# SwiGLU gate/up in a hybrid decoder step: seven-product scheme with chained PSUM accumulation

## The chip, the cores and the metric

The kernel runs on one core of one Trainium2 chip. The metric is the device time of one execution in microseconds, as the median over runs. Engines are called by their names or as the profile abbreviates them: TensorE (PE for matmuls, PEld for its weight loads), VectorE (DVE), ScalarE (ACT), GpSimd (POOL) and SyncE (SP), which issues the DMAs.

## The reference, cut to what matters

One decoder layer over 2048 prompt tokens and 8 sample tokens, width D = 1024, all in fp32. The change touches only the middle of its second half, the gate and up products of the feed-forward block:

```python
def swiglu(h, w_gate, w_up, w_down):
    return (jax.nn.silu(h @ w_gate) * (h @ w_up)) @ w_down
xp = xp + swiglu(rmsnorm(xp, norm2_g[l]), w_gate[l], w_up[l], w_down[l])   # D_FF = 2816
```

## The kernel before, in words

The program is a chain of stages with a barrier between them: input projections, attention, output projection (`combine`), gate and up (`gate_up`, line 2363 on), and down (`down`). Each stage hands the engines their own instruction streams; within a stage everything is ordered by semaphores written out by hand.

**Seven products for eight.** `gate_up` computes each block product by a Strassen-Winograd scheme. The 2056 tokens are split into three passes (`WIDTHS` 344, 344, 340, each for two halves of tokens), the 1024 inputs into two halves, and the output columns are taken two blocks of 128 at a time. One *item* g is such a pair of column blocks of w_gate (even g) or of w_up (odd g): 22 items a pass, 66 in all. An item has seven products, each a 512-deep sum: b11, b21 and b22 use blocks of the weights as they are, t1 to t4 use sums and differences of blocks, made by GpSimd (`combos`, lines 2545 to 2556). The token side uses four blocks and the combinations S1 to S4. Each operand is split in two fp32r parts, hi (a ScalarE copy) and lo (a VectorE or GpSimd difference), and a product is hi*hi + hi*lo + lo*hi: 12 matmuls of 128x344 (lines 2826 to 2828), so 84 an item.

**What is made of them.** With p1 = b11, u2 = p1 + t2, u3 = u2 + t3 and u4 = u2 + t1, the four output quarters are c11 = p1 + b21, c22 = u3 + t1, c21 = u3 + t4 and c12 = u4 + b22. Before, each product has a PSUM bank of its own, taken in turn from eight (`product_bank`). ScalarE copies b11 out of PSUM (line 2647, p1, double buffered); VectorE makes u2 (line 2747), u3 (2757), u4 (2766) and the quarters (2699), every one with one PSUM input. For a gate item ScalarE turns the quarters into silu of them (2656 to 2662). For an up item VectorE multiplies each quarter by the gate's (2703) and makes three sums and two differences for the down stage (2712 to 2720); SyncE then stores them, three or four DMAs of sums (2530) and as many of quarters (2533).

**The order of the queues.** TensorE goes through the items in `ORDER`; every product waits, one item behind, for the reader of the bank that it takes over. In iteration g ScalarE does `base_hi(g+1)` (the hi parts of plain blocks, which waits for item g-1 to be over), the p1 copy, `combos_hi(g+1)` (line 2600, waits for GpSimd's t_made), then the silus of a gate item. VectorE does u2, `combos_lo(g+1)` (2677), `base_lo(g+1)` (2687), u3 and the quarters. GpSimd does `base_lo(g+1)` (2567, 2570, 2571) and `combos(g+2)`, which waits for VectorE's `combos_lo(g+1)`. Before a gate item's c11 VectorE waits for the stores of the sums of the pair before (sum_stored), before an up item's first quarter for those of its quarters (stored).

**The turns.** In the last item of a pass (g = 21 and 43) the token operands are exchanged: ScalarE makes seven new hi parts (`tokens_hi`, line 2632), VectorE seven lo parts (`tokens_lo`, line 2692) between its other work, and GpSimd the last combination S4 (line 2472). SyncE loads the raw tokens of the next pass in item 5 of a pass (`load_tokens`, line 2315, four DMAs of 680 to 688 KB), in its queue between the weight loads and the stores of that item.

**The start.** For item 0 the hi and lo parts are made within the stage. ScalarE's loop over items begins only after all seven token parts, so the p1 copy of item 0 comes after `base_hi(1)`. The weight combinations of item 1 lie in the tile `lead`, whose end is also u3.

The numbers of `T` in this text: T(g) is the start of the first matmul of item g.

Of the kernel before, what the change touches and what calls it, by code (L numbers as in the profile page):

```python
# [25 lines left out]
P = 128  # L26
# [2221 lines left out]
ORDER = ("b11", "t2", "t3", "t1", "b21", "t4", "b22")  # L2248
SLOT = {"t2": 0, "t3": 1, "t1": 2, "t4": 3}
# [113 lines left out]
def gate_up(nc, c, io, scratch, raw, stock, lead):  # L2363
# [20 lines left out]
    with ExitStack() as ctx:  # L2384
# [4 lines left out]
        first = stock[:, 12 * FW + 5 * D - 2 * W:12 * FW + 5 * D].rearrange("p (b t) -> p b t", b=2)  # L2389
# [3 lines left out]
        u2 = sb("u2", [P, 2, W])  # L2393
# [5 lines left out]
        source_of = (A11, S2, S3, S1, A12, A22, S2)  # L2399
        names = ("w_in0 w_in1 t_step t_made t_hi t_lo b_hi b_lo d_lo a11_in h_in s_step h_hi h_lo b_first done p1 u2 u3 u4 c22 c11 c21 c12 silu "  # L2400
                 "quarter summed act stored sum_stored s_stored ahead t2_hi t2_lo tail_in tail_var tail_rooted root_out root_in tail_turned tail_step tail_out")
        with stage(nc, names) as (block, s):
            w_in = (s.w_in0, s.w_in1)

            def source(sc, m):

                return part[:, source_of[m] if sc or m < M - 1 else A11, :, 0:WIDTHS[sc]]
# [25 lines left out]
            def product_bank(g, name):  # L2433
                return ps[:, (M * g + ORDER.index(name)) % 8, :]
# [18 lines left out]
            def s_combo(eng, sc, name):  # L2453
# [14 lines left out]
                else:  # L2468

                    eng.wait_ge(s.s_step, step + 3)  # L2470
                    eng.wait_ge(s.h_lo, M * sc + 1)
                    eng.tensor_tensor(x[S2], x[A12], x[S2], ALU.subtract).then_inc(s.s_step, 1)
# [114 lines left out]
            def _(act):  # L2587
                def combos_hi(g):
# [6 lines left out]
                    if g == 0:  # L2595
                        act.activation(w_hi[0][:, 0], combo[:, 0], ACT.Copy).then_inc(s.t2_hi, 1)
# [22 lines left out]
                def tokens_hi(sc, m):  # L2619

                    n = WIDTHS[sc]
                    if sc and m == 6:
                        act.wait_ge(s.s_step, 4 * sc)
                    elif sc and m == 0:
                        act.wait_ge(s.a11_in, 16 * sc)
                    elif sc and m in (4, 5):
                        act.wait_ge(s.h_in, 48 * sc)
                    elif sc:
                        act.wait_ge(s.s_step, 4 * sc - 4 + {1: 2, 2: 3, 3: 1}[m])
# [3 lines left out]

                combos_hi(0)
                for m in (2, 3):
                    tokens_hi(0, m)
                base_hi(0)
                for m in range(4, M):
                    tokens_hi(0, m)
                for g in range(N):  # L2640
                    n, b = width(g), g % 2
                    if g + 1 < N:
                        base_hi(g + 1)
                    act.wait_ge(s.done, done(g, "b11"))
                    if g >= 2:
                        act.wait_ge(s.c11, g - 1)
                    act.activation(first[:, b, 0:n], product(g, "b11"), ACT.Copy).then_inc(s.p1, 1)
                    if g + 1 < N:
                        combos_hi(g + 1)
                    if is_up(g):  # L2650
                        if g % ITEMS == ITEMS - 1 and g // ITEMS + 1 < SC:
                            for m in range(M):
                                tokens_hi(g // ITEMS + 1, m)
                        continue
                    act.wait_ge(s.c22, g + 1)
                    act.activation(sil[:, 3, 0:n], sil[:, 3, 0:n], ACT.Silu).then_inc(s.silu, 1)
                    act.wait_ge(s.c11, g + 1)
                    act.activation(sil[:, 0, 0:n], sil[:, 0, 0:n], ACT.Silu).then_inc(s.silu, 1)
                    act.wait_ge(s.c21, g + 1)
                    act.activation(sil[:, 1, 0:n], sil[:, 1, 0:n], ACT.Silu).then_inc(s.silu, 1)  # L2660
                    act.wait_ge(s.c12, g + 1)
                    act.activation(sil[:, 2, 0:n], sil[:, 2, 0:n], ACT.Silu).then_inc(s.silu, 1)
# [695 lines left out]
```

## Time and profile before

| what | us |
|---|---|
| runs, median of 3 (lowest, highest) | 2722.22 (2721.59, 2729.13) |
| profiled execution, span from first to last instruction | 2721.9 |
| TensorE matmul busy | 2609.9 (96%) |
| VectorE, GpSimd, ScalarE busy | 1878.3, 1726.6, 1196.8 |
| the gate/up stage, first to last matmul | 1366.2 to 2263.1 |
| mean granted TensorE clock | 0.988 of full |

The profile gives no device time of the profiled execution apart from its span. Matmuls are pipelined: a 128x344 matmul is shown as 320 ns, but one starts every 157 ns, so a stretch in which "PE busy" equals its length has no hole, and a hole shows as missing busy time or as a matmul that starts late. The granted clock (PEclk) is a share of 2.4 GHz; at half of it the matmuls start every 287 ns.

### The profile page before, as it was taken

The page shows a single profiled execution, that of the slowest core. Times are in us where ns is not written, and L with a number is a line of the kernel's source. Part 1 is how long each engine was busy: PE and PEld are TensorE (multiplying, and loading weights), DVE is VectorE, ACT ScalarE, POOL GpSimd, SP SyncE. Part 2 cuts the span into 40 slices and gives each one's busy share as a digit, 9 for nine tenths or more (in the row PEclk, how much of TensorE's full clock was granted, in tenths as well). Part 3 has the DMA queues.
Part 4 walks back from the last instruction along what each step waited for, and adds up shares of the span by engine and source line. Part 5 has one row for each costly group of instructions (what it writes and reads, how often), then busy time and mean ns, then how long its engine had stood idle before and what let it go on. Part 6 is the DMA issues. An engine that isn't in the chain of part 4 may idle for free. (4 is left out here: it accounts for less than half of the span.)

```text
span 2721.9 us, 42328 instructions
## 1 busy us (share of the span) xinstructions
PE 2609.9 (96%) x14706; PEld 2358.5 (87%) x14706; DVE 1878.3 (69%) x2513; ACT 1196.8 (44%) x2106; POOL 1726.6 (63%) x1004
## 2 busy tenths in 40 slices
PE   8999999989999998899989999999999998999998
PEld 7999898877787777787789998999999997888887
DVE  5366687488888888632387888787887784455564
ACT  4222321377777778744453334333433332232343
POOL 3387687489999999665656776677656660222232
PEclk9999999999999999999999999999999999999999
DMA  6588898666667677775636343534345536755564
GB/s 207 176 257 253 265 293 290 180 181 183 177 179 192 184 181 181 237 259 184 200 106 174 115 132 114 173 115 132 114 124 149 154 106 200 245 171 178 182 228 139
DMA packets 471718, 497.17 MB, mean 183 GB/s; under 512 B 173179, under 2 KB 360566, under 8 KB 470474
## 3 DMA queue, kind: packets, MB, share of 16 engines
q1 hardware_dynamic: 450722, 468.96, 57.4%
q10 hardware_dynamic: 20496, 24.45, 2.6%
q8 instruction: 118, 1.93, 0.3%
q0 software_dynamic: 288, 1.05, 0.1%
q14 instruction: 94, 0.77, 0.1%
HBM read 397.06 MB, written 94.16 MB: 180 GB/s over the span
## 5 line engine op out<-in xcount | busy, mean ns | idle before, releaser
L2826 PE MATMUL ps_gate_up<-h_hi,w_hi 128*128 128x344 f32 (+1 forms) x1584 | 509.0, 321 | 15.4 <-DVE h_lo L2692 14.6
L2827 PE MATMUL ps_gate_up<-h_lo,w_hi 128*128 128x344 f32 (+1 forms) x1584 | 507.2, 320 | 0.0
L2828 PE MATMUL ps_gate_up<-h_hi,w_lo 128*128 128x344 f32 (+1 forms) x1584 | 506.6, 320 | 0.0
L2826 PEld LDWEIGHTS ps_gate_up<-h_hi,w_hi 128*128 128x128 f32 x1584 | 299.1, 189 | 18.3 <-DVE h_lo L2692 16.5
L2828 PEld LDWEIGHTS ps_gate_up<-h_hi,w_lo 128*128 128x128 f32 x1584 | 299.4, 189 | 0.0
L2827 PEld LDWEIGHTS ps_gate_up<-h_lo,w_hi 128*128 128x128 f32 x1584 | 299.1, 189 | 0.0
L881 PE MATMUL ps_proj<-w_hi,h_lo 128*128 128x428 f32 (+1 forms) x800 | 284.6, 356 | 0.0
L1601 DVE TENSOR_TENSOR split_halves<-ps_turned,split_halves 128x512 fp32r<-128x512 f32 (+1 forms) x352 | 210.7, 614 | 65.3 <-ACT split_halves L1485 62.9
L3020 POOL TENSOR_TENSOR stock<-common 128x512 f32<-128x512 f32 x55 | 84.0, 1537 | 264.7 <-DMA common<-in_w_down 264.6
L2551 POOL TENSOR_TENSOR stock<-common 128x512 f32<-128x512 f32 x64 | 103.4, 1616 | 230.5 <-DVE w_lo L2677 230.5
L3222 PE MATMUL ps_down<-wd_hi,split_halves 128*128 128x512 f32 x616 | 241.1, 391 | 7.3 <-DVE wd_lo L3130 7.2
L3223 PE MATMUL ps_down<-wd_lo,split_halves 128*128 128x512 f32 x616 | 240.5, 390 | 0.0
L3224 PE MATMUL ps_down<-wd_hi,act_lo 128*128 128x512 f32 x616 | 240.3, 390 | 0.0
L1485 ACT ACTIVATE split_halves<-ps_turned 128x512 fp32r<-128x512 f32 (+1 forms) x352 | 185.8, 538 | 110.9 <-PE ps_turned L1424 96.6
L3068 ACT ACTIVATE split_halves<-stock 128x768 fp32r<-128x768 f32 (+2 forms) x114 | 83.2, 776 | 302.5 <-PE ps_down L3224 288.6
L1424 PE MATMUL ps_turned<-ident,probs 128*128 128x128 f32 x1216 | 195.3, 278 | 15.7 <-DVE split_halves L1601 9.9
L3146 DVE TENSOR_TENSOR acc<-acc,ps_down 128x512 f32<-128x512 f32 x96 | 62.3, 684 | 201.3 <-PE ps_down L3224 201.3
L1424 PEld LDWEIGHTS ps_turned<-ident,probs 128*128 128x128 f32 x1216 | 144.7, 142 | 59.9 <-DVE split_halves L1601 23.1
L2677 DVE TENSOR_TENSOR w_lo<-stock,w_hi 128x2048 fp32r<-128x2048 f32 x64 | 158.9, 2483 | 24.4 <-ACT w_hi L2600 24.4
L528 POOL TENSOR_TENSOR stock<-stock,q_row 128x2048 f32<-128x2048 f32 x32 | 156.5, 4896 | 28.4 <-DMA stock<-in_cache_k 28.3
L730 DVE TENSOR_REDUCE part_scores<-stock 128x32 f32<-128x2048 f32 x48 | 109.4, 2285 | 88.7 <-POOL stock L528 88.1
L1333 POOL TENSOR_TENSOR common<-common,lead 128x2048 f32<-128x2048 f32 x43 | 156.1, 3631 | 18.6 <-DMA common<-in_cache_v 18.6
(407 smaller groups left out, 7280.0 us busy)
## 6 DMA issues: line engine op xcount, KB each, us to landing
stock<-in_cache_k SPq DMA_DIRECT2D x192, 256.0 KB, 3.5
common<-in_cache_v SPq DMA_DIRECT2D x172, 256.0 KB, 3.1
stock<-act_combined SPq DMA_DIRECT2D x56, 704.0 KB, 4.3
common<-in_w_gate SPq DMA_DIRECT2D x33, 1024.0 KB, 5.3
common<-in_w_up SPq DMA_DIRECT2D x33, 1024.0 KB, 6.8
common<-in_w_down SPq DMA_DIRECT2D x44, 512.0 KB, 5.9
page_v<-in_cache_v SPq DMA_DIRECT2D x84, 256.0 KB, 3.0
common<-in_w_in SPq DMA_DIRECT2D x44, 428.0 KB, 4.7
```

The costliest lines, as they stand in the source:

```text
L528: pool.tensor_tensor(part, part, query, ALU.mult).then_inc(s.pool_done, 1)
L881: mm = pe.matmul(ps[:, bank, 0:w], a_lo, w_hi[:, d, :], start=False, stop=(j == 3 and d == 1))
L1424: turned = pe.transpose(out[:, r * P:(r + 1) * P], probs(u.head, QCH * u.ch + r, u.j * P, (u.j + 1) * P), c.ident[:])
L1485: act.activation(a.p_hi[:, m % PARTS, r0 * P:], ps_t[:, bank_of["unit", m], r0 * P:], ACT.Copy).then_inc(s.t_hi, 1)
L1601: dve.tensor_tensor(a.p_lo[:, m % PARTS, r0 * P:], ps_t[:, bank_of["unit", m], r0 * P:], a.p_hi[:, m % PARTS, r0 * P:].bitcast(F32), ALU.s ...
L2677: dve.tensor_tensor(shape(w_lo[g % 2][:, 0:4]), shape(combos_second if g == 1 else combo), shape(w_hi[g % 2][:, 0:4]).bitcast(F32), ALU.su ...
L2826: pe.matmul(acc, a_hi, h_hi[:, d, :], start=d == 0, stop=False)
L2827: pe.matmul(acc, a_hi, h_lo[:, d, :], start=False, stop=False)
L2828: mm = pe.matmul(acc, a_lo, h_hi[:, d, :], start=False, stop=d == H - 1)
L3222: pe.matmul(out, a_hi[:, n % 2, j, :], w_hi[:, slot, :], start=first, stop=False)
L3223: pe.matmul(out, a_hi[:, n % 2, j, :], w_lo[:, slot, :], start=False, stop=False)
L3224: mm = pe.matmul(out, a_lo[:, n % 2, j, :], w_hi[:, slot, :], start=False, stop=end)
```

## The change

The products come in another order, and sums that VectorE made are left to the accumulation in PSUM: t2 is added onto the bank of b11, t3 onto that of t2, and b22 onto that of t1. ScalarE copies the bank of b11 out three times: after b11 (p1), after t2 (u2) and after t3 (u3). The sum u4 is gone, since t1 + b22 now comes out of one bank. Items take bank 0 to 3 or 4 to 7 in turn. p1 is single now. A product that adds onto a bank waits for the reader of the same item: t2 for p1, t3 for u2, b22 for VectorE's c22. The other four wait two items behind. In the last item of a pass the token parts are spread between the p1, u2 and u3 copies on ScalarE, and on VectorE from ahead of `combos_lo` to the end. For a gate item the wait for sum_stored now stands ahead of c11 and c22, and c11 comes first. The token combination S4 is written to another part (A11).

```diff
-ORDER = ("b11", "t2", "t3", "t1", "b21", "t4", "b22")
+ORDER = ("b11", "t1", "t2", "b21", "t3", "t4", "b22")
+BANK = {"b11": 0, "t2": 0, "t3": 0, "t1": 1, "b22": 1, "b21": 2, "t4": 3}
+ADDS = {"t2": "b11", "t3": "t2", "b22": "t1"}
...
-                return ps[:, (M * g + ORDER.index(name)) % 8, :]
+                return ps[:, 4 * (g % 2) + BANK[name], :]
...
# ScalarE
                     act.wait_ge(s.done, done(g, "b11"))
-                    if g >= 2:
-                        act.wait_ge(s.c11, g - 1)
-                    act.activation(first[:, b, 0:n], product(g, "b11"), ACT.Copy).then_inc(s.p1, 1)
+                    if g >= 1:
+                        act.wait_ge(s.c11, g)
+                    act.activation(p1[:, 0:n], product(g, "b11"), ACT.Copy).then_inc(s.p1, 1)
+                    if turn:
+                        tokens_hi(turn, 0)
                     if g + 1 < N:
                         combos_hi(g + 1)
+                    act.wait_ge(s.done, done(g, "t2"))
+                    if g == 0:
+                        act.wait_ge(s.t_lo, 2)
...
+                    act.activation(u2[b][:, 0:n], product(g, "t2"), ACT.Copy).then_inc(s.u2, 1)
+                    if turn:
+                        for m in (1, 2):
+                            tokens_hi(turn, m)
+                    act.wait_ge(s.done, done(g, "t3"))
+                    if g >= 1:
+                        act.wait_ge(s.c21, g)
+                    act.activation(u3[:, 0:n], product(g, "t3"), ACT.Copy).then_inc(s.u3, 1)
+                    if turn:
+                        for m in range(3, M):
+                            tokens_hi(turn, m)
...
# VectorE
-                    dve.tensor_tensor(u2[:, b, 0:n], product(g, "t2"), first[:, b, 0:n], ALU.add).then_inc(s.u2, 1)
                     if g + 1 < N:
                         combos_lo(g + 1)
                         base_lo(g + 1)
+                    if turn:
+                        tokens_lo(turn, 1)
...
-                    dve.tensor_tensor(u3[:, 0:n], u2[:, b, 0:n], product(g, "t3"), ALU.add).then_inc(s.u3, 1)
...
+                    else:
+                        dve.wait_ge(s.sum_stored, stored_before(q))
+                    dve.wait_ge(s.p1, g + 1)
+                    quarter(g, "b21", p1[:, 0:n], 0, s.c11)
+                    dve.wait_ge(s.u3, g + 1)
                     quarter(g, "t1", u3[:, 0:n], 3, s.c22)
-                    dve.tensor_tensor(u2[:, b, 0:n], u2[:, b, 0:n], product(g, "t1"), ALU.add).then_inc(s.u4, 1)
...
# TensorE
-                        if m == 0 and g >= 2:
-                            pe.wait_ge(s.c12, g - 1)
-                        if m >= 1:
-                            pe.wait_ge((s.p1, s.u2, s.u3, s.u4, s.c11, s.c21)[m - 1], g)
+                        if name in ADDS:
+                            pe.wait_ge({"t2": s.p1, "t3": s.u2, "b22": s.c22}[name], g + 1)
+                        elif g >= 2:
+                            pe.wait_ge({"b11": s.u3, "t1": s.c12, "b21": s.c11, "t4": s.c21}[name], g - 1)
...
-                            pe.matmul(acc, a_hi, h_hi[:, d, :], start=d == 0, stop=False)
+                            pe.matmul(acc, a_hi, h_hi[:, d, :], start=d == 0 and name not in ADDS, stop=False, skip_group_check=name in ADDS)
```

## Rows read from the trace of the kernel before

**Rows 1.** The page's first part: busy time of each engine over the span.
```profile
PE 2609.9 (96%) x14706; PEld 2358.5 (87%) x14706; DVE 1878.3 (69%) x2513; ACT 1196.8 (44%) x2106; POOL 1726.6 (63%) x1004
```

**Rows 2.** Windows: stretch, length, busy us of PE, PEld, DVE, ACT, POOL, clock, DMA.
```profile
1660.00:1680.00 20.00, 13.29 (x65) 12.24 (x64) 19.69 (x19) 6.42 (x7) 10.98 (x5) 0.78 0.16 51
...
1700.00:1900.00 200.00, 200.00 (x1277) 200.00 (x1276) 159.05 (x207) 73.50 (x103) 138.74 (x87) 1.00 0.49 144
...
1960.00:1980.00 20.00, 12.35 (x68) 11.26 (x66) 19.69 (x19) 7.14 (x7) 11.72 (x5) 0.91 0.15 49
```

**Rows 3.** Timeline of TensorE: first matmul of items 0, 1, 6, 20, 21, 23.
```profile
1366.23 0.63 PE L2826 MATMUL ps_gate_up<-split_halves 128*128 128x344 f32 x1 [6.00 <-PEq L84]
1382.90 0.32 PE L2826 MATMUL ps_gate_up<-split_halves,w_hi 128*128 128x344 f32 x1
1450.14 0.32 PE L2826 MATMUL ps_gate_up<-split_halves 128*128 128x344 f32 x1
1635.69 0.32 PE L2826 MATMUL ps_gate_up<-split_halves 128*128 128x344 f32 x1
1648.87 0.32 PE L2826 MATMUL ps_gate_up<-split_halves,w_hi 128*128 128x344 f32 x1
1686.08 0.32 PE L2826 MATMUL ps_gate_up<-split_halves,w_hi 128*128 128x344 f32 x1
```

**Rows 4.** Groups by line in the stage: busy us, mean ns; idle before.
```profile
L2747 DVE TENSOR_TENSOR u<-ps_gate_up,stock 128x344 f32<-128x344 f32 (+1 forms) x66 | 33.8, 511 | 99.3 <-PE ps_gate_up L2828 78.3 <-ACT stock L2647 21.1
L2757 DVE TENSOR_TENSOR lead<-u,ps_gate_up 128x344 f32<-128x344 f32 (+1 forms) x66 | 33.1, 501 | 0.9 <-PE ps_gate_up L2828 0.9
L2766 DVE TENSOR_TENSOR u<-u,ps_gate_up 128x344 f32<-128x344 f32 (+1 forms) x66 | 33.1, 501 | 0.0
L2647 ACT ACTIVATE stock<-ps_gate_up 128x344 f32<-128x344 f32 (+1 forms) x66 | 29.4, 445 | 8.2 <-PE ps_gate_up L2828 8.2
```

**Rows 5.** Timeline of item 29 (up): its first matmul; ScalarE; VectorE.
```profile
1765.16 0.32 PE L2826 MATMUL ps_gate_up<-split_halves,w_hi 128*128 128x344 f32 x1
1767.94 0.43 ACT L2647 ACTIVATE stock<-ps_gate_up 128x344 f32<-128x344 f32 x1
1768.27 1.91 ACT L2600 ACTIVATE w_hi<-stock 128x2048 fp32r<-128x2048 f32 x1
1772.73 0.68 DVE L2687 TENSOR_TENSOR w_lo<-common,w_hi 128x512 fp32r<-128x512 f32 x1
1783.87 0.52 DVE L2720 TENSOR_TENSOR lead<-lead 128x344 f32<-128x344 f32 x1
```

**Rows 6.** Timeline of the stage's start: ScalarE's first p1 copy, VectorE's `combos_lo(1)`.
```profile
1378.19 0.46 ACT L2647 ACTIVATE stock<-ps_gate_up 128x344 f32<-128x344 f32 x1
1380.49 4.00 DVE L2677 TENSOR_TENSOR w_lo<-lead,w_hi 128x2048 fp32r<-128x2048 f32 x1
```

**Rows 7.** Timeline around item 6: token loads, stores of sums, VectorE's c11 quarter.
```profile
1448.43 5.62 SPq L2315 DMA_DIRECT2D stock<-h_turned  x4
1456.95 3.09 SPq L2530 DMA_DIRECT2D act_combined<-lead  x3
1465.67 0.51 DVE L2699 TENSOR_TENSOR lead<-stock,ps_gate_up 128x344 f32<-128x344 f32 x1 [4.13 <-DMA act_combined<-lead]
```

**Rows 8.** Timeline of the first turn: TensorE, VectorE, ScalarE, GpSimd.
```profile
1670.29 0.42 PE L2826 MATMUL ps_gate_up<-h_hi,w_hi 128*128 128x344 f32 x1 [4.20 <-DVE h_lo L2692]
1675.92 0.65 PE L2826 MATMUL ps_gate_up<-h_hi,w_hi 128*128 128x344 f32 x1 [2.52 <-DVE h_lo L2692]
1665.43 3.29 DVE L2712 TENSOR_TENSOR lead<-lead 128x344 f32<-128x344 f32 x1
1684.99 0.68 DVE L2687 TENSOR_TENSOR w_lo<-common,w_hi 128x512 fp32r<-128x512 f32 x1
1664.99 3.36 POOL L2472 TENSOR_TENSOR stock<-stock 128x1376 f32<-128x1376 f32 x1
1671.11 0.43 ACT L2647 ACTIVATE stock<-ps_gate_up 128x344 f32<-128x344 f32 x1
```

More of the change, by code:

```diff
@@ L2641, in _ @@
                     n, b = width(g), g % 2
+                    turn = g // ITEMS + 1 if g % ITEMS == ITEMS - 1 and g // ITEMS + 1 < SC else 0
                     if g + 1 < N:
@@ L2650, in _ @@
+                    act.wait_ge(s.done, done(g, "t3"))
[3 more added lines that the diff above has]
+                    if turn:
+                        for m in range(3, M):
+                            tokens_hi(turn, m)
                     if is_up(g):
-                        if g % ITEMS == ITEMS - 1 and g // ITEMS + 1 < SC:
-                            for m in range(M):
-                                tokens_hi(g // ITEMS + 1, m)
@@ L2662, in _ @@
-                    act.activation(sil[:, 2, 0:n], sil[:, 2, 0:n], ACT.Silu).then_inc(s.silu, 1)
+                    gated(g, 0, s.c11)
+                    gated(g, 3, s.c22)
+                    gated(g, 1, s.c21)
+                    gated(g, 2, s.c12)
             @block.vector
@@ L2734, in _ @@
                 combos_lo(0)
-                for m in (2, 3):
-                    tokens_lo(0, m)
+                tokens_lo(0, 2)
                 base_lo(0)
-                for m in range(4, M):
+                for m in range(3, M):
                     tokens_lo(0, m)
@@ L2750, in _ @@
                         base_lo(g + 1)
[L2751 removed]
+                    if turn:
+                        tokens_lo(turn, 1)
                     if g == 1:
                         sample_turned()
[L2754 to L2760 removed]
                     if is_up(g):
@@ L2764, in _ @@
                             dve.wait_ge(s.s_stored, 16 * (q - (SC - 1) * PAIRS))
+                    else:
+                        dve.wait_ge(s.sum_stored, stored_before(q))
+                    if g == 0:
+                        dve.wait_ge(s.t_lo, 2)
+                    dve.wait_ge(s.p1, g + 1)
+                    quarter(g, "b21", p1[:, 0:n], 0, s.c11)
+                    dve.wait_ge(s.u3, g + 1)
                     quarter(g, "t1", u3[:, 0:n], 3, s.c22)
-                    dve.tensor_tensor(u2[:, b, 0:n], u2[:, b, 0:n], product(g, "t1"), ALU.add).then_inc(s.u4, 1)
                     if turn:
-                        tokens_lo(turn, 1)
-                    if not is_up(g):
-                        dve.wait_ge(s.sum_stored, stored_before(q))
-                    quarter(g, "b21", first[:, b, 0:n], 0, s.c11)
+                        tokens_lo(turn, 2)
                     if is_up(g):
@@ L2774, in _ @@
                     if turn:
-                        tokens_lo(turn, 2)
+                        tokens_lo(turn, 3)
                     quarter(g, "t4", u3[:, 0:n], 1, s.c21)
@@ L2779, in _ @@
                     if turn:
-                        tokens_lo(turn, 3)
-                    dve.wait_ge(s.u4, g + 1)
-                    quarter(g, "b22", u2[:, b, 0:n], 2, s.c12)
+                        tokens_lo(turn, 4)
+                    dve.wait_ge(s.u2, g + 1)
+                    quarter(g, "b22", u2[b][:, 0:n], 2, s.c12)
                     if is_up(g):
@@ L2785, in _ @@
                     if turn:
-                        for m in range(4, M):
+                        for m in range(5, M):
                             tokens_lo(turn, m)
@@ L2806, in _ @@
                             pe.wait_ge(s.d_lo, 1)
[L2807 removed]
+                        if g == 1 and name == "t1":
                             pe.wait_ge(s.t_lo, 2)
```

78 lines of the change are left out of this document (34 added, 44 removed).

## The prediction

> **What bounds the kernel now.** I began with the page: TensorE is busy 96% of the span, VectorE 69%, ScalarE 44% [rows 1]. The change lies in one stage, so I cut that stage into windows. In the middle of a pass 200 us hold 200.00 us of matmuls while VectorE is busy 159 us and ScalarE 73.5 us: there is no hole, and a matmul starts every 157 ns [rows 2]. An item lasts 13.18 us (item 20 to item 21) [rows 3], so each of its seven products has 1.88 us. Holes lie only where a pass turns: 6.7 and 7.6 us of two windows of 20 us, with VectorE busy 19.7 us of each and a granted clock of 0.78 and 0.91 [rows 2]. The first turn, T(21) to T(23), takes 37.21 us where two items need 26.36 [rows 3]: 10.85 us too many. So TensorE bounds the stage, and VectorE bounds its turns. What is taken from VectorE in mid-pass is worth nothing; the question is whether TensorE's new waits, on the reader of the same item instead of one an item back, are met.
>
> **What the change removes and adds.** It removes u2, u3 and u4 from VectorE, 66 each of 511, 501 and 501 ns [rows 4]: 99.9 us. It adds 132 copies to ScalarE at the 445 ns of the p1 copy [rows 4]: 59 us. The number of matmuls and of TensorE's waits is the same. With no hole in mid-pass, all this is hidden by TensorE, provided that the next part holds.
>
> **Mid-pass: do the three new waits hold?** I take item 29, an up item, from T = 1765.16 [rows 5]. Product k starts at T + 1.88 k (k from 0), and its first weight load 0.2 earlier.
> - t2 (k = 2) is due to start at 3.77, and needs p1. The copy ends at 1768.37, T + 3.21 [rows 5], and nothing ahead of it on ScalarE changes. 0.35 to spare.
> - t3 (k = 4) is due at 7.53 and needs u2. ScalarE is through with `combos_hi` at T + 5.02 [rows 5], t2 is over at 5.9, the copy ends at 6.35. 1.0 to spare.
> - b22 (k = 6) is due at 11.30 and needs c22, which needs u3: t3 over at 9.65, copy to 10.1, c22 to 10.6. VectorE has finished `base_lo` at T + 8.25 [rows 5], does c11 and its product by 9.4, and waits for u3. 0.5 to spare.
>
> In a gate item the wait for the stores comes ahead of c22. VectorE's work of an up item now ends at T(30) + 6.05 (1784.39) [rows 5]; three operations fewer make it some 4.5, so sums land sooner too. I cost mid-pass at 0; the cover is those 0.35 and 0.5 us.
>
> **The start: +7.8 us, and perhaps 1.0 of clock.** In item 0 p1 stands behind all token parts and `base_hi(1)` on ScalarE and ends at 1378.65 [rows 6]. The before kernel doesn't care, because nothing of item 0 needs it; now t2, the third product, waits for it. Next ScalarE's u2 copy waits for t_lo = 2, the end of `combos_lo(1)`: 1380.49 + 4.00 = 1384.49 [rows 6]. So u2 ends at 1384.95, and t3, t4 and b22 follow: 3 x 1.88, T(1) = 1390.7. It was 1382.90 [rows 3]: +7.8. TensorE idles 6.5 us before t2, 2.5 before t3. At a turn the hole of 4.2 us [rows 8] stands in the window with clock 0.78 [rows 2]. At half clock t3, t4 and b22 would add 12 x 130 ns each, 4.7 us; the second turn's 0.91 says less. I take 1.0, bounds 0 and 4.7.
>
> The Trainium skill (TensorE: Matmul & The Clock Gate, Part 1) says that idleness takes the array to half of its 2.4 GHz and only sustained work brings it back. By it the 4.7 would stand in full, and the sum would be 3.7 us higher. The trace agrees in kind (0.78 and 0.91 at the turns), not on the amount.
>
> **What the start gives back: -2.4 us.** Items 1 to 20 take 1648.87 - 1382.90 = 265.97 us, where 20 x 13.18 = 263.6 [rows 3]. The 2.4 us is lost because GpSimd, VectorE and ScalarE run behind TensorE after the start. With TensorE 7.8 us later they are not behind.
>
> **Item 6: +4.1 us.** The token loads occupy SyncE for 5.62 us and the DMA queues for longer. The stores of sums behind them are issued at 1456.95, and VectorE waited 4.13 us for them, to 1465.67 [rows 7], which is T(6) + 15.5 [rows 3]. That hid behind TensorE, as c22 had gone ahead of the wait and only c11 was late. Now c11 and c22 both stand behind it, and b22 of the same item needs c22, due at T + 11.3. The stores may be issued up to 2 us sooner, but the token loads are ahead of them; c11 starts between T + 13.7 and 15.5, b22 1.1 later: 3.5 to 5.3 us of waiting. I take 4.1; the lower bound is 0, should the stores land at once. At item 28 I saw no such wait, and cost it at 0.
>
> **The turns: +0.8 each.** VectorE is the chain. `base_lo(23)` ends at 1685.67, T(21) + 36.8 [rows 8]. Three 0.5 us operations fall out of the chain and it starts 0.5 earlier, with `tokens_lo(0)`: 35.0. But then c11 and c22 of item 22 follow (1.0), and only then may b22 start (1.9): T(23) at T(21) + 37.9, against 37.2. Inside, ScalarE makes a second wait. S4 ends on GpSimd at T(21) + 19.5, the last token part and the p1 copy of item 22 come behind it, to 22.7 [rows 8]. As `tokens_lo(0)` now stands ahead of `combos_lo(22)`, GpSimd starts 1.4 later, and t2 of item 22 can't start before 24.2 (the third product started at 21.4 [rows 8]). At full clock four products bring TensorE to 31.7, in time for c22 at 36.0; at half clock, 3.44 us each, to 38.0, and T(23) would be 4 us late. I take 0.8, 1.6 for both; bounds -4 and +4 a turn.
>
> **The sum.** 7.8 + 1.0 - 2.4 + 4.1 + 1.6 = +12.1 us. The profiled span of 2721.9 becomes 2734.0; the median of the runs is 0.3 above that span. I forecast 2734, 0.4% slower. A measurement of this kernel can tell about 0.3%, 8.2 us, from no change.
>
> **Rivals.**
> - *The mid-pass waits miss.* An operation with both inputs in SBUF takes VectorE 0.52 us alone [rows 5] and 3.29 beside GpSimd [rows 8]. If such lengthening costs c22 more than the 0.5 to spare, by 0.3 to 0.6 us in each of 33 up items, it adds 10 to 20: about 2749. For it: the margin is thin. Against: item 29 already has GpSimd running beside it. Chance 0.12.
> - *The turns at half clock.* 3.2 more at each turn: 2740 and, with a slow start, up to 2745. Chance 0.12.
> - *No change that can be told.* The stores of item 6 land early (-4.1) and the turns gain 1 to 3 us each because VectorE's lengthened operations fall differently beside GpSimd: 2721.9 + 12.1 - 4.1 - 1.6 - 4 = 2724. Chance 0.20.
> - *Faster, by the turns.* VectorE at 19.7 of 20 us is what makes the holes, and the change takes work from just this engine. If its chain shrank until the turns had no hole, they would give back 2 x 10.85: 8.8 - 2.4 + 4.1 - 21.7 = -11.2, 2711. It decides at T(21) to T(23) below 27.9 us; the other terms are +10.5, and 8.2 more must come from two turns. Against it: three operations are 1.5 us, and only contention with GpSimd (3.29 against 0.52) could give the rest. Chance 0.06.
>
> The Trainium skill (SBUF — State Buffer, § Who interferes with whom) says that a VectorE instruction with two SBUF inputs contends with a GpSimd one that reads SBUF, and one with at most one doesn't. The removed operations read one input from PSUM and keep to 0.50 us; by that rule all lengthened ones stay, which speaks against the last rival.
>
> That the change doesn't do what it says would show as adds left on VectorE; the diff leaves none.
>
> **How the numbers follow.** The forecast itself (2728 to 2740) has 0.50. Slower than 2730.4: 0.46 of that and the two slower rivals, 0.70. Within 0.3%: the rest of the forecast and the third rival, 0.24. Faster: 0.06. The range 2724 to 2748 leaves out the faster rival, a part of the third and the worst of the first.
>
> **What would show it.** T(1) near 1390.7, with a hole before item 0's third product that ends with ScalarE's copy, and one before its fifth. A hole of 3.5 to 5.3 us before b22 of item 6. Mid-pass windows still full. T(21) to T(23) near 38, with t2 of item 22 waiting for ScalarE. I am wrong if mid-pass windows show holes, if T(1) moves by less than 6, or if a turn takes under 34 us.

## The result, and the profile after

The changed kernel takes 2746.88 us (median of 5 runs, 2744.22 to 2747.71), the kernel before beside it 2722.22 (2718.83 to 2729.13). The ratio is 1.0093, interval 1.0082 to 1.0105: 24.7 us slower, where 12.1 was forecast. The profiled execution took 2747.01 us with a span of 2745.3.

The page's first part, after:
```profile
PE 2620.0 (95%) x14706; PEld 2366.1 (86%) x14706; DVE 1803.7 (66%) x2315; ACT 1254.4 (46%) x2238; POOL 1715.0 (62%) x1004
```
Against [rows 1] VectorE lost 74.6 us of busy time, ScalarE gained 57.6. The work moved as meant; that bought nothing. Added up one by one, VectorE's operations in the stage fell by 90.0 us and not by the 99.9 of the three groups, since others got longer, above all its products with the gate's quarters (115.4 to 146.8 us). The page counts time in which two operations overlap once, and so shows less still.

The window in mid-pass of [rows 2], after (columns as there), then the first turn:
```profile
1700.00:1900.00 200.00, 198.08 (x1253) 197.23 (x1253) 137.01 (x155) 84.13 (x127) 129.22 (x85) 0.99 0.46 135
1662.00:1700.00 38.00, 27.85 (x152) 26.49 (x151) 32.91 (x27) 17.49 (x20) 21.82 (x12) 0.89 0.30 88
```
The first line matters: 1277 matmuls before, 1253 after. TensorE has holes in mid-pass, though VectorE is less busy (137 for 159 us).

First matmuls of items 0, 1, 6, 7, 21 and 23, after, which answer to [rows 3]:
```profile
1362.66 0.63 PE L2840 MATMUL ps_gate_up<-split_halves 128*128 128x344 f32 x1 [6.17 <-PEq L84]
1387.47 0.32 PE L2840 MATMUL ps_gate_up<-split_halves,w_hi 128*128 128x344 f32 x1
1453.79 0.32 PE L2840 MATMUL ps_gate_up<-split_halves 128*128 128x344 f32 x1
1473.28 0.39 PE L2840 MATMUL ps_gate_up<-split_halves,w_hi 128*128 128x344 f32 x1
1659.01 0.32 PE L2840 MATMUL ps_gate_up<-split_halves,w_hi 128*128 128x344 f32 x1
1699.98 0.49 PE L2840 MATMUL ps_gate_up<-split_halves,w_hi 128*128 128x344 f32 x1
```
T(g) is again the start of the first matmul of item g, T1-T0 the time from T(0) to T(1). Over all 66 items, in sections, each row from the one profiled execution of its kernel (us; e1 to e9 are the experiments below; "stage" is from the start of the first to the start of the last matmul of gate and up):

| | T1-T0 | T21-T1 | T23-T21 | T43-T23 | T45-T43 | T65-T45 | stage |
|---|---|---|---|---|---|---|---|
| before | 16.7 | 266.0 | 37.2 | 263.6 | 36.9 | 263.2 | 896.6 |
| after | 24.8 | 271.5 | 41.0 | 268.3 | 40.4 | 264.8 | 923.8 |
| e1 | 24.7 | 267.9 | 38.9 | 263.6 | 39.9 | 263.6 | 911.6 |
| e2 | 23.4 | 271.4 | 40.6 | 267.2 | 40.7 | 264.0 | 920.3 |
| e3 | 24.7 | 271.6 | 37.8 | 269.0 | 38.2 | 265.9 | 920.1 |
| e4 | 24.8 | 271.9 | 39.5 | 267.0 | 40.6 | 264.3 | 921.0 |
| e5 | 17.1 | 267.4 | 37.6 | 265.5 | 37.9 | 264.0 | 902.6 |
| e6 | 17.1 | 267.2 | 37.6 | 265.7 | 37.9 | 264.0 | 902.6 |
| e7 | 17.1 | 267.3 | 42.7 | 265.6 | 43.0 | 264.0 | 912.7 |
| e8 | 16.7 | 265.9 | 41.7 | 263.6 | 42.3 | 263.2 | 906.2 |
| e9 | 16.7 | 267.8 | 37.1 | 263.7 | 37.4 | 263.2 | 898.8 |

The stage grew by 27.2 us. It began 3.6 us earlier in the profiled execution of after; no instruction ahead of it differs, and over the eleven kernels that start lies anywhere from 1361.8 to 1372.4. So a single device time carries up to some 10 us that has nothing to do with the edit. I read the stage, and use device times only where several executions stand behind them.

Where the 27.2 us lie, item by item: the start +8.1; items 1 to 20 (without item 6 and the three of mid-pass among them) no longer pay the start's delay, -1.9; item 6 +6.3; nine items in mid-pass (10, 14, 18, 28, 32, 36, 40, 54, 62) +6.1; the first turn with item 23 +4.7, the second with item 45 +3.8.

Waits over the stage of after, four of them (engine and line, for whom it waited: us in all, times, longest):
```profile
DVE lead L2718 <- DMA act_combined<-lead: 31.0, 30, 6.2
PE ps_gate_up L2840 <- DVE lead L2718: 19.8, 11, 4.6
DVE lead L2718 <- ACT lead L2672: 13.8, 35, 1.8
PE ps_gate_up L2840 <- ACT stock L2653: 11.4, 3, 6.2
```
The same view of before has one wait of this sort:
```profile
DVE lead L2699 <- DMA act_combined<-lead: 4.1, 1, 4.1
```
VectorE now waits for the stores of sums in 30 gate items. TensorE waits eleven times for VectorE's c22: seven times behind such a wait (items 6, 28, 32, 36, 40, 54, 62), and four times at the turns (items 21, 22, 43, 44), where other work of VectorE stands ahead of c22. In items 10, 14 and 18 its pause is so short (0.1 us) that the view leaves it out.

**Mid-pass.** Item 28, a gate item, T(28) = 1766.85; VectorE's last sum of item 27 and its c11, SyncE's stores, ScalarE's u3 copy, TensorE's b22 and T(29):
```profile
1772.37 0.52 DVE L2739 TENSOR_TENSOR lead<-lead 128x344 f32<-128x344 f32 x1
1778.04 0.51 DVE L2718 TENSOR_TENSOR lead<-stock,ps_gate_up 128x344 f32<-128x344 f32 x1 [2.35 <-DMA act_combined<-lead]
1778.47 0.93 DVE L2718 TENSOR_TENSOR lead<-lead,ps_gate_up 128x344 f32<-128x344 f32 x2
1772.91 1.99 SPq L2533 DMA_DIRECT2D act_combined<-lead  x4
1776.47 0.46 ACT L2672 ACTIVATE lead<-ps_gate_up 128x344 f32<-128x344 f32 x1 [3.30 <-PE ps_gate_up L2842]
1779.03 0.42 PE L2840 MATMUL ps_gate_up<-h_hi,w_hi 128*128 128x344 f32 x1 [0.72 <-DVE lead L2718]
1781.01 0.32 PE L2840 MATMUL ps_gate_up<-split_halves,w_hi 128*128 128x344 f32 x1
```
The sums of item 27 are ready at T(28) + 6.04, their stores land 5.1 us after that, at T + 11.2; c11 and c22 stand behind them, and b22, due at T + 11.3, starts at T + 12.2. ScalarE's copy, on which I had spent my attention, was done at T + 10.1.

The nine items are of two kinds. In 28, which like item 6 has token loads ahead of its stores, and in 54 and 62 the sums are ready at T + 6.0, as in most gate items, but the last store lands at T + 10.8 to 11.2, where 9.2 to 10.2 is usual. In 10, 14, 18, 32, 36 and 40, which hold 3.8 of the 6.1 us, it is the sums that are late, by 1.3 us (T + 7.3), and the stores land at T + 10.6 to 11.1. In just these six one sum of VectorE takes 2.68 us beside GpSimd; in every other pair of items it takes 0.52. The same sum in items 29 and 31, then c11 of item 32:
```profile
1795.41 0.52 DVE L2733 TENSOR_TENSOR lead<-lead 128x344 f32<-128x344 f32 x1
1822.58 2.68 DVE L2733 TENSOR_TENSOR lead<-lead 128x344 f32<-128x344 f32 x1
1831.63 0.51 DVE L2718 TENSOR_TENSOR lead<-stock,ps_gate_up 128x344 f32<-128x344 f32 x1 [0.93 <-DMA act_combined<-lead]
```
The six are each the second item behind one in which GpSimd makes S1, S2 or S3 (items 8, 12 and 16 of the first two passes; the third pass has none). That this work is what puts GpSimd beside the sum fits all six items, and no run took it away.

**Item 6**, T(6) = 1453.79: token loads, stores, VectorE's c11, TensorE's b22 (answers to [rows 7]):
```profile
1451.56 6.26 SPq L2317 DMA_DIRECT2D stock<-h_turned  x4
1459.87 3.23 SPq L2533 DMA_DIRECT2D act_combined<-lead  x3
1468.83 0.51 DVE L2718 TENSOR_TENSOR lead<-stock,ps_gate_up 128x344 f32<-128x344 f32 x1 [6.18 <-DMA act_combined<-lead]
1469.82 0.51 PE L2840 MATMUL ps_gate_up<-h_hi,w_hi 128*128 128x344 f32 x1 [4.57 <-DVE lead L2718]
```
c11 starts at T + 15.0, b22 at T + 16.0, 4.7 late, and then takes 3.46 us for its 12 matmuls (to 1473.28) where 1.88 is usual: half clock.

**The start**, T(0) = 1362.66: TensorE's t2; ScalarE's p1 and u2 copies (answers to [rows 6]):
```profile
1375.22 0.62 PE L2840 MATMUL ps_gate_up<-h_hi,w_hi 128*128 128x344 f32 x1 [6.21 <-ACT stock L2653]
1374.62 0.46 ACT L2653 ACTIVATE stock<-ps_gate_up 128x344 f32<-128x344 f32 x1
1381.01 0.46 ACT L2665 ACTIVATE stock<-ps_gate_up 128x344 f32<-128x344 f32 x1 [4.13 <-DVE w_lo L2696]
```

**The first turn**, T(21) = 1659.01 (answers to [rows 8]): holes of TensorE before b22 of item 21, t2 and b22 of item 22 (a fourth, 1.4 us before t4, is left out); then VectorE from `tokens_lo(0)` to c22 of item 22, in part; then GpSimd's S4 and ScalarE's p1 copy of item 22:
```profile
1673.37 0.42 PE L2840 MATMUL ps_gate_up<-h_hi,w_hi 128*128 128x344 f32 x1 [2.90 <-DVE lead L2718]
1683.34 0.39 PE L2840 MATMUL ps_gate_up<-h_hi,w_hi 128*128 128x344 f32 x1 [2.49 <-ACT stock L2653]
1696.41 0.62 PE L2840 MATMUL ps_gate_up<-h_hi,w_hi 128*128 128x344 f32 x1 [3.10 <-DVE lead L2718]
...
1663.50 2.47 DVE L2711 TENSOR_TENSOR split_halves<-stock,split_halves 128x1376 fp32r<-128x1376 f32 x1 [3.71 <-ACT split_halves L2634]
1674.33 2.67 DVE L2711 TENSOR_TENSOR h_lo<-stock,h_hi 128x1376 fp32r<-128x1376 f32 x1
1676.91 3.46 DVE L2731 TENSOR_TENSOR lead<-lead 128x344 f32<-128x344 f32 x1
1695.76 0.93 DVE L2718 TENSOR_TENSOR lead<-lead,ps_gate_up 128x344 f32<-128x344 f32 x2
...
1675.50 4.50 POOL L2475 TENSOR_TENSOR stock<-stock 128x1376 f32<-128x1376 f32 x1
...
1682.76 0.44 ACT L2653 ACTIVATE stock<-ps_gate_up 128x344 f32<-128x344 f32 x1
```
VectorE works without a gap from 1663.50 on. The last operation ahead of c11 and c22, `base_lo(23)`, ends at T(21) + 36.4, c22 a microsecond later, and b22 of item 22 follows at half clock: 1696.41 to T(23) = 1699.98 is 3.57 us for 12 matmuls.

### The profile page after: what moved, and what is told of

Its sections match the earlier page's. It is cut to its first block and busy times, and to the rows that moved or that the text cites. A ratio compares the mean times of both kernels' runs of the same rounds, so it can differ in the third digit from the quotient of the medians.

```text
span 2745.3 us, 42296 instructions
## 1 busy us (share of the span) xinstructions
PE 2620.0 (95%) x14706; PEld 2366.1 (86%) x14706; DVE 1803.7 (66%) x2315; ACT 1254.4 (46%) x2238; POOL 1715.0 (62%) x1004
## 5 line engine op out<-in xcount | busy, mean ns | idle before, releaser
L3034 POOL TENSOR_TENSOR stock<-common 128x512 f32<-128x512 f32 x55 | 85.4, 1563 | 264.2 <-DMA common<-in_w_down 264.0
L528 POOL TENSOR_TENSOR stock<-stock,q_row 128x2048 f32<-128x2048 f32 x32 | 159.1, 4980 | 23.5 <-DMA stock<-in_cache_k 23.4
L1333 POOL TENSOR_TENSOR common<-common,lead 128x2048 f32<-128x2048 f32 x43 | 156.1, 3629 | 18.7 <-DMA common<-in_cache_v 18.6
```

Of the source, the lines that this page charges most:

```text
L528: pool.tensor_tensor(part, part, query, ALU.mult).then_inc(s.pool_done, 1)
```

## The experiments

Each experiment sets two theories against one another. Theory A is one throughout: the added time is made of new waits, each of which can be taken out by itself: c22 behind the wait for stores (mid-pass, item 6), the copies behind other work (start), and VectorE's chain with c22 at its end (turns). Theory B, the rival, was formed anew for each. A ratio is to the kernel before, run beside it on the same chip; e2, e3, e4, e6 and e9 had one execution each, so for them only the stage is read.

**e1: c22 ahead of the wait for the stores**, on the changed kernel.
```
                     if is_up(g):
                         ...
                     else:
+                        dve.wait_ge(s.u3, g + 1)
+                        quarter(g, "t1", u3[:, 0:n], 3, s.c22)
                         dve.wait_ge(s.sum_stored, stored_before(q))
-                    ...
                     dve.wait_ge(s.p1, g + 1)
                     quarter(g, "b21", p1[:, 0:n], 0, s.c11)
-                    dve.wait_ge(s.u3, g + 1)
-                    quarter(g, "t1", u3[:, 0:n], 3, s.c22)
```
(In up items c11 stays ahead of c22.)

> The changed kernel, but in gate items VectorE makes c22 first and only then waits for the stores of the sums, ahead of c11. Theory A (the store wait costs TensorE time because c22 stands behind it): the holes of the changed kernel before b22 in items 6 (4.9 us), 10, 14, 18, 28, 32, 36, 40, 54, 62 (0.4 to 1.0 us each) go, item 6 takes 13.2 us instead of 19.5, and the execution is some 12 us shorter than the changed kernel's (about 2735). At the turns c22 comes one quarter sooner, 0.4 us each. Rival B (those holes come from VectorE running late as such, the lengthened operations with two SBUF inputs): the holes stay within 0.4 us of what they were except in item 6, and no more than 6 us are won.

Measured: 2736.1 us (median of 5), ratio to before 1.0054 (1.0033 to 1.0076); the stage is 12.2 us shorter than after's. All holes before b22 in mid-pass are gone, and item 6 takes 13.18 us. The same window; then c11 of item 6 and the one hole that is left near it:
```profile
1700.00:1900.00 200.00, 200.00 (x1277) 200.00 (x1275) 146.05 (x164) 83.15 (x125) 132.11 (x85) 1.00 0.48 139
...
1467.94 0.51 DVE L2718 TENSOR_TENSOR lead<-stock,ps_gate_up 128x344 f32<-128x344 f32 x1 [4.47 <-DMA act_combined<-lead]
...
1472.07 0.65 PE L2844 MATMUL ps_gate_up<-h_hi,w_hi 128*128 128x344 f32 x1 [2.10 <-ACT stock L2653]
```
The window is full again, 1277 matmuls. The late c11 of item 6 now holds p1's single buffer, so t2 of item 7 waits for the copy: item 7 takes 17.05 us, and 3.8 of the 6.3 us won are given back, which the expectation did not have. Item 6 and mid-pass are shown to be this one wait: 8.6 of the 12.2 us. The other 3.5 lie at the turns, 3.0 of them at the first: c22 came 0.4 us sooner there, as expected, and b22 behind it ran at full clock (1.98 us for 3.58), which was not expected.

**e2: p1 and u2 of item 0 copied between the token parts** on ScalarE, instead of behind them all.
```
                 base_hi(0)
+                act.activation(p1[:, 0:W], product(0, "b11"), ACT.Copy)...
+                for m in (3, 4): tokens_hi(0, m)
+                act.activation(u2[0][:, 0:W], product(0, "t2"), ACT.Copy)...
-                for m in range(3, M): tokens_hi(0, m)
+                for m in (5, 6): tokens_hi(0, m)
```


> The changed kernel, but in item 0 ScalarE makes the p1 copy right after the hi parts of the first plain blocks, and the u2 copy after two further token parts; the wait for combos_lo(1) is left at the u3 copy alone. Theory A (two waits in a row set the start: p1 behind all token parts, then the wait for combos_lo(1)): the 6.5 us hole before t2 goes, but b22 of item 0 now waits for u3 and c22 behind combos_lo(1), so that T(0) to T(1) is about 21.9 us against 24.8 in the changed kernel and 16.7 before. Rival B (the late p1 copy is the whole cost): T(0) to T(1) comes back to 17 or 18 us.

Measured: T1-T0 is 23.4 for 24.8, where A expected 21.9 and B 17 to 18. TensorE's largest hole of item 0:
```profile
1392.20 0.63 PE L2847 MATMUL ps_gate_up<-h_hi,w_hi 128*128 128x344 f32 x1 [4.46 <-DVE lead L2725]
```
The 6.2 us hole before t2 has become one of 4.5 before b22, which waits for c22, which stands on VectorE behind `combos_lo(1)`. Theory A's mechanism holds: two waits stand behind one another, and taking the first uncovers the second. The 1.5 us over its 21.9 are clock: b22 behind the hole took 3.58 us for 1.88. (This execution took 2753.94 us; its stage began 9.7 us later than after's.)

**e3: in the first item of a pass c11 and c22 ahead of `combos_lo` of the next item.**
```
-                    if g + 1 < N:
+                    fresh = g > 0 and g % ITEMS == 0
+                    if g + 1 < N and not fresh:
                         combos_lo(g + 1); base_lo(g + 1)
                     ...
                     quarter(g, "t1", u3[:, 0:n], 3, s.c22)
+                    if fresh:
+                        combos_lo(g + 1); base_lo(g + 1)
```


> The changed kernel, but in items 22 and 44 VectorE makes c11 and c22 ahead of combos_lo and base_lo of the next item. Theory A (the turn ends late because b22 of the first item of a pass waits for c22 behind the whole of VectorE's chain): T(21) to T(23) falls from 40.97 to about 37.6 us, and the second turn by as much; what remains is bounded by base_lo(23). Rival B (the turn is set by ScalarE's p1 copy behind the last token part, and by TensorE at half clock): less than 1 us is won at each turn.

Measured: the turns shorten by 3.1 and 2.2 us (A expected 3.4 each, B less than 1), and the stage by only 3.7. The one execution took 2747.09 us, no less than the 2746.88 of after; its stage began 3.0 us later. TensorE behind the turn:
```profile
1696.77 0.39 PE L2844 MATMUL ps_gate_up<-h_hi,w_hi 128*128 128x344 f32 x1 [0.63 <-DVE lead L2718]
1699.69 0.40 PE L2844 MATMUL ps_gate_up<-split_halves,w_hi 128*128 128x344 f32 x1 [0.78 <-DVE w_lo L2706]
```
The hole before b22 falls to 0.63; then item 23's first product waits for `base_lo`, and its b22 0.5 us for c22. So the order of VectorE's work sets which of TensorE's products waits. Of the 5.3 us that the turns won 1.6 are lost again, above all in items 24, 45 and 46, which take 0.9, 0.5 and 0.5 us more.

**e4: p1 of a pass's first item ahead of the last token part** on ScalarE.
```
-                        for m in range(3, M):
+                        for m in range(3, M - 1):
                             tokens_hi(turn, m)
                 ...  (next item, behind its p1 copy)
+                    if g and g % ITEMS == 0:
+                        tokens_hi(g // ITEMS, M - 1)
```


> The changed kernel, but ScalarE makes the last token part (which waits for S4 of GpSimd) after the p1 copy of items 22 and 44 and not before it. Theory A (VectorE's chain ends the turn): the 2.8 us hole before t2 of item 22 goes, TensorE waits longer before b22 instead, and T(21) to T(23) stays within 0.7 us of 40.97. Rival B (the p1 copy behind S4 is what makes the turn longer): T(21) to T(23) falls by 2.5 to 3 us.

Measured: first turn 39.5 (-1.5), second 40.6 (+0.2); the first fits neither A (within 0.7) nor B (2.5 to 3 less). The one execution took 2746.89 us, as after. The hole before t2 is gone, the one before b22 is still 3.1:
```profile
1698.54 0.40 PE L2842 MATMUL ps_gate_up<-h_hi,w_hi 128*128 128x344 f32 x1 [3.08 <-DVE lead L2720]
```
b22 starts 23.19 us after b22 of item 21 here (1675.35 to 1698.54), and 23.04 in after (1673.37 to 1696.41): the end of the turn has not moved. What the first turn won is clock: b22 of item 22 took 1.97 us (to T(23) = 1700.51) for 3.57, and 17 matmuls in the turn came at half clock (some 287 ns apart) in place of 36. The profile has the granted clock at half from 1695.3 to 1702.1 in after, over that b22, and no such stretch there in e4; the second turn won nothing. The hole before t2 costs nothing by itself; VectorE's chain ends the turn.

**e5: all of them together**: e1, e3 and e4; the token loads of item 5 issued behind its stores; and item 0's copies early with c22 of item 0 ahead of `combos_lo(1)` (kept in `act_out`, u3 in u2's odd buffer):
```
-                    if g % ITEMS == 5 and g // ITEMS + 1 < SC:
-                        tokens(g // ITEMS + 1)
                     ...
                     (stores of sums and quarters)
+                    if g % ITEMS == 5 and g // ITEMS + 1 < SC:
+                        tokens(g // ITEMS + 1)
```


> The changed kernel with c22 ahead of the store wait in gate items, c11 and c22 of items 22 and 44 ahead of combos_lo, the last token part behind the p1 copy, the token loads issued behind the stores of item 5 of a pass, and a start in which p1, u2 and u3 of item 0 are copied as soon as their product is done (u3 into the tile of u2_odd, c22 into act_out, since lead still holds the combinations of item 1). Theory A (every loss of the changed kernel is one of these four waits): item 0 takes 16.9 to 18.5 us instead of 24.8, items 6 and 7 take 13.2 each, mid-pass items show no hole, T(21) to T(23) is about 37.5, and the stage's first to last matmul is 896 to 901 us as before (896.6) against 923.8; the execution is within 0.3% of the kernel before. Rival B (ScalarE's copies or TensorE's waits cost something by themselves, spread over the items): the stage stays above 906 us although these waits are gone.

Measured: 2730.98 us (median of 8), ratio 1.0034 (1.0021 to 1.0047); stage 902.6. That is 21.2 of the 27.2 us, won by taking out four waits. A expected 896 to 901 and B above 906; A's account holds for four fifths of the loss, and the rest falls between the two. It stays 6 us longer than before's: 0.4 at the start, 1.4 in items 1 to 20 (item 1's t2 waits 1.9 us for p1), 0.4 and 1.0 at the turns, 1.9 and 0.8 in the sections behind them. Whether e5 is within 0.3% of before, as A expected, the interval leaves open.

**e6: e5 with c11 and c22 of a pass's last item ahead of `tokens_lo(1)`**, to see whether b22 of that item matters.
```
-                    if turn:
-                        tokens_lo(turn, 1)
                     ... (c11, c22)
                     if turn:
+                        tokens_lo(turn, 1)
                         tokens_lo(turn, 2)
```


> The kernel e5_all_mended, and in the last item of a pass VectorE makes c11 and c22 ahead of the second token part. Theory A (a turn is as long as VectorE's chain, so where TensorE waits in it doesn't matter): the 3.0 us hole before b22 of items 21 and 43 shrinks to under 1 us, later holes grow, and T(21) to T(23) stays within 0.7 us of that of e5_all_mended. Rival B (each hole of a turn is a loss of its own): T(21) to T(23) falls by 2 to 3 us.

Measured: 2726.89 us (one execution); turns 37.59 and 37.89 for 37.64 and 37.94, as A expected. TensorE's hole before b21 of item 22:
```profile
1671.23 0.66 PE L2874 MATMUL ps_gate_up<-h_hi,w_hi 128*128 128x344 f32 x1 [4.85 <-DVE h_lo L2731]
```
The one before b22 of item 21, 2.88 us in e5, is 0.30 here; this one, 1.62 in e5, is 4.85. What the one hole lost the other gained, and the turn is as long as before, which fits a turn that VectorE's chain ends.

**e7: e6 with the last two lo halves of the tokens on GpSimd**, which in after lay idle for 9.3 us of the turn; 3.1 us less on VectorE's chain.
```
+            def pool_part(eng, sc, m):
+                eng.wait_ge(s.h_hi, M * sc + m)
+                eng.tensor_tensor(h_part(m, 1, n), source(sc, m), h_part(m, 0, n)..., ALU.subtract)
...
+                            pool_part(pool, sc, 5)      (behind S4)
+                        pool_part(pool, g // ITEMS, 6)  (next item, behind base_lo)
-                        for m in range(5, M):
-                            tokens_lo(turn, m)
```


> The kernel e6_c22_ahead_of_part, and at each turn GpSimd makes the lo halves of the last two token parts, which takes 3.1 us out of VectorE's chain. Theory A (VectorE's chain is the length of a turn): T(21) to T(23) falls from 37.6 to 34 to 35.5 us, both turns together win 4 to 7 us, and the kernel comes level with the kernel before or some 0.1% under it. Rival B (GpSimd's and VectorE's operations lengthen each other by as much as is moved): less than 1 us a turn.

Measured: 2738.78 us (median of 5), ratio 1.0055 (1.0042 to 1.0068). A expected turns 2 to 3.6 us shorter, B a gain of less than 1; they got longer by 5.1 us each, to 42.7 and 43.0, which neither had. TensorE's holes in them still end with lo halves that VectorE makes (5.6 and 4.2 us in the first), none with one of GpSimd's. VectorE and GpSimd in the same stretch of e7:
```profile
1670.30 4.49 DVE L2747 TENSOR_TENSOR h_lo<-stock,h_hi 128x1376 fp32r<-128x1376 f32 x1
1674.71 0.50 DVE L2758 TENSOR_TENSOR lead<-lead,ps_gate_up 128x344 f32<-128x344 f32 x1
1675.24 2.16 DVE L2762 TENSOR_TENSOR lead<-lead 128x344 f32<-128x344 f32 x1
1677.43 3.30 DVE L2773 TENSOR_TENSOR lead<-lead 128x344 f32<-128x344 f32 x1
1680.76 0.52 DVE L2775 TENSOR_TENSOR lead<-lead 128x344 f32<-128x344 f32 x1
...
1669.96 3.37 POOL L2436 TENSOR_TENSOR h_lo<-stock,h_hi 128x1376 fp32r<-128x1376 f32 x1
1673.29 3.73 POOL L2583 TENSOR_TENSOR w_lo<-common,w_hi 128x1024 fp32r<-128x1024 f32 x1
```
While GpSimd runs, the same product of 128x344 takes VectorE 2.16 us and the sum 3.30; as soon as GpSimd stops (a third operation, of 3.38 us, ends at 1680.35) a sum takes 0.52. The token half behind the first sum takes 4.49, in after 1.58.

**e8: the same move on the kernel before.** Was it the move, or something of the changed kernel?

> The kernel before, with the same move of two lo halves a turn from VectorE to GpSimd and nothing of the change. Theory A: T(21) to T(23) falls from 37.2 to 34 to 35 us, the execution by 4 to 6 us, about 0.2%, and it is the fastest of all kernels here, since the chained accumulation buys nothing at the turns. Rival B: no gain, as above.

Measured: 2734.51 us (median of 6), ratio 1.0046 (1.0033 to 1.0059); turns 41.7 and 42.3, longer by 4.4 and 5.4. The same operations take the same time:
```profile
1668.08 4.49 DVE L2708 TENSOR_TENSOR h_lo<-stock,h_hi 128x1376 fp32r<-128x1376 f32 x1
1673.02 2.16 DVE L2719 TENSOR_TENSOR lead<-lead 128x344 f32<-128x344 f32 x1
1675.22 3.29 DVE L2730 TENSOR_TENSOR lead<-lead 128x344 f32<-128x344 f32 x1
```
So it is the move: in the changed kernel and in the old one, the 3.1 us taken from VectorE cost it more than they saved.

**e9: the kernel before, with its wait for the stores ahead of c22**, as the changed kernel has it.
```
+                    if not is_up(g):
+                        dve.wait_ge(s.sum_stored, stored_before(q))
                     quarter(g, "t1", u3[:, 0:n], 3, s.c22)
                     ...
-                    if not is_up(g):
-                        dve.wait_ge(s.sum_stored, stored_before(q))
                     quarter(g, "b21", first[:, b, 0:n], 0, s.c11)
```


> The kernel before, but in gate items the wait for the stores of the sums stands ahead of c22, as in the changed kernel. Theory A (the wait costs only because b22 adds onto the bank that c22 reads, in the same item): VectorE waits about as often for the stores as in the changed kernel, TensorE's matmuls stay without a hole in mid-pass, and the stage stays within 1 us of 896.6 except for up to 2 us at items 6 and 7. Rival B (the position of the wait costs as such): holes as in the changed kernel, 10 us and more.

Measured: 2723.82 us (one execution); stage 898.8, +2.2: 1.9 in items 7 to 10, the rest at the turns. They stand behind this wait in item 6, for which the profile names no releaser; in the program the wait for the stores stands there:
```profile
1463.28 0.51 DVE L2699 TENSOR_TENSOR lead<-lead,ps_gate_up 128x344 f32<-128x344 f32 x1 [6.18 <-issue]
```
There is no hole in mid-pass beyond these. In the kernel before, the position of the wait costs some 2 us; in the changed kernel, where b22 adds onto the bank that c22 reads, it costs 12.4 (item 6 and mid-pass). One part of the expectation missed: VectorE waited noticeably in only three items, for 9.2 us, and not in 30 for 31.0, as its operations fall at other times there. So the two numbers do not come from the same waits, and how much of the difference is the accumulation alone is not shown.

## Why the prediction was right and wrong

*Sign and bound: right; size: half.* Measured were 24.7 us where 12.1 were forecast. The terms that were too small are the turns (by 6.9 us), mid-pass (by 6.1) and item 6 (by 2.2). TensorE bounds the stage, work taken from VectorE in mid-pass is worth nothing, and only new waits count.

*The start: right in sum, wrong in its parts.* Predicted 7.8 + 1.0, measured 8.1. The hole before t2 was 6.2 (6.5 predicted). The one of 2.5 before t3 did not come: TensorE ran t2 and most of b21 ahead of it at half clock, and the copy (u2 ended at T(0) + 18.8) was there in time. From t2 to T(1) five products took 12.25 us, 2.85 over five times 1.88; the clock took the place of the hole.

*The give-back: right.* -1.9 for -2.4.

*Item 6: hole right, clock forgotten.* c11 at T + 15.0 was within 13.7 to 15.5. But I costed half clock behind the start's hole and not behind this one: 1.6 us. With a hole of 4.7 for 4.1 that makes 6.3.

*Mid-pass, costed at 0: wrong, +6.1.* The step was "three operations fewer make it some 4.5, so sums land sooner too". In a usual gate item the sums were ready at T + 6.0, as before (6.05). t3 had moved from third to fifth product; its copy ends at T + 10.1, c22 waits for it (35 waits, 13.8 us), and that idle time used up what the three operations saved. The landing time of the stores I never worked out for a usual item. In after the last store lands 3.2 to 4.2 us behind the sums (in items 28, 54 and 62 4.8 to 5.1), so at T + 10.6 to 11.1 in the six items where the sums are 1.3 us late. From there c11 and c22 take another 1.0 us, and b22 is due at T + 11.3. The trace of before could have told it: the sums were ready at T + 7.5 and their stores landed at T + 11.2 to 11.3 in items 32, 36 and 40, but I had looked at items 28 and 29 alone. I gave the three waits on ScalarE 0.35, 1.0 and 0.5 us to spare, found them sufficient, and they were. The fourth, VectorE's wait for a DMA, had its margin unmeasured, since in the kernel before nothing in the same item hung on it.

The rival "the mid-pass waits miss" came near in time (2749), in part by luck: it wanted c22 late by lengthened operations in 33 up items, 10 to 20 us. Measured were 6.1 us in nine gate items, where c22 waited for stores; in six of them a lengthened sum is why the stores were late.

*The turns: +1.6 predicted, +8.5 measured* (with items 23 and 45 behind them). The first: 37.9 predicted for T23-T21, 41.0 measured, in two steps. "35.0" for the end of `base_lo(23)` was 36.4. (The working, 36.8 less three operations of 0.5 less 0.5, gives 34.8.) VectorE's two-input operations fell differently beside GpSimd, which was itself later: over what they took in before, `tokens_lo(0)` was 0.2 us longer, `tokens_lo(1)` 0.4, `tokens_lo(2)` 1.1, the first sum 0.2, and `combos_lo(22)` 0.3 shorter. And b22 of item 22 took 3.57 us for 1.9, at half clock behind a 3.1 us hole. The item after it lost 1.0 more. At the second turn b22 of item 44 took 3.17. The wait on ScalarE stood where I put it (copy end T + 24.2 for 24.1), but by luck: S4 began 0.4 us later than before, not 1.4, and took 4.50 us for 3.36. e4 showed that this wait does not end the turn. The bound of +4 a turn held the first (+3.8 by T23); the value that I took did not, because it priced b22 behind its wait at the full rate, 1.9 us. The rival "the turns at half clock" had the size (3.2 more a turn; by T(23) and T(45) it was 3.0 and 2.7 more), and about half of it by its own mechanism: it wanted four products at half clock, and it was one, at the end of a chain that was itself 1.4 us late.

The prediction cited the Trainium skill (TensorE: Matmul & The Clock Gate, Part 1): idleness takes the array to half clock, and sustained work brings it back. The trace agrees: at the start TensorE ran t2 and most of b21 at half clock and the rest at full, at item 6 and at the first turn all of b22 at half (3.46 and 3.57 us). That half clock would then hold for every product behind the hole was my reading and not the page's: the five from t2 on took 12.25 us, not 17.2. And behind the hole of 3.08 us in e4 b22 ran at full rate. A value between the bounds was right; mine was too near the lower one.

*Contention.* Every 128x344 operation of VectorE with one input in PSUM took 0.49 to 0.52 us in all runs, also in the midst of e7's stretch, while its neighbours went to 2.16 and 3.30. This agrees with the rule that the prediction cites from the Trainium skill (SBUF — State Buffer, § Who interferes with whom): VectorE with two SBUF inputs contends with GpSimd, with one it doesn't.

## What to carry to other kernels

When a chain of accumulation waits for a reader in the same item, list everything that stands ahead of that reader on its engine, DMA waits included, and work out when each is met in a *usual* item; a wait that cost nothing may only have been covered by what did not hang on it. Price a hole in TensorE's work as the hole plus what half clock costs behind it: here nothing in e4, 1.6 us behind item 6, 2.7 behind the first turn (b22 and item 23), 2.9 at the start. And before work is moved to an idle GpSimd, add up what the two-input operations of VectorE beside it will cost: here 3.1 us moved lengthened the section by 4.4 to 5.4.

## What the runs showed of the hardware that I had not expected

- VectorE's 128x344 operation on two SBUF inputs takes 0.52 us alone; beside GpSimd many take 1.07 and some up to 3.47. The 128x1376 half takes 1.58 alone, up to 2.27 beside it in before, 2.69 in after and 4.49 in e7 and e8. Not every one gets longer. GpSimd's own S4 took 3.36 us in before and 4.50 in after. e7 and e8 made the section longer by giving GpSimd a share.
- Behind holes of 2.1 to 6.2 us the matmuls came some 287 ns apart instead of 157: 34 to 36 of them at the start and at each turn of after, 13 behind item 6; before had 16, 24 and 14 at the start and the turns. The 2.1 us are the hole in item 7 of e1, with no other of over 0.3 us for 80 us ahead of it: the granted clock was half from 1472.0 to 1475.4, over the product behind it.
- The start of the stage wandered by 10 us between executions, with the code ahead of it unchanged, while sections of the stage that an edit left alone came back within some 1.1 us (T23 to T43 of after and e2: 268.3 and 267.2). A single item can move more: item 6 took 19.5, 17.7, 18.6 and 18.9 us in after, e2, e3 and e4, none of which touched it.

**What stays open.** No version beat the kernel before: e5 is 1.0034 times its time, and e6 had one execution (2726.89). A turn with GpSimd kept idle beside VectorE's chain was not tried, nor sums of a pass's last item put off past the turn, nor a second buffer for p1, nor a mid-pass without GpSimd's S1 to S3 beside VectorE's sums. Why the last stores land late in items 54 and 62 was not looked into. Why the second turn won no clock in e4, where the first did, and so why one hole of 3.1 us brings half clock and another not, was not settled.
